# Gated linear attention in a two-layer trunk: the decay of all tokens made during the projections and loaded by chunk

## What is computed

```python
proj = h @ w_in                          # q, k (4 heads x 128), v, g_out (1024 each), a_lr (16)
log_a = log_sigmoid(a_lr @ w_gate2 + b_gate) / 16
# by chunk of tokens, per head:
bcum = cumsum(log_a, within the chunk)
o_inter = (q * exp(bcum)) @ state
attn[t, s] = sum_d q[t, d] * k[s, d] * exp(bcum[t, d] - bcum[s, d])     # s <= t
o = o_inter + attn @ v
k_dec = k * exp(bcum[last] - bcum)
state = exp(bcum[last]) * state + k_dec.T @ v
y = rms_norm(o) * silu(g_out) @ w_out
```

## Time and profile before

| | |
|---|---|
| median of 3 runs | 2583.39 us (2582.79 to 2583.41) |
| the profiled execution | 2580.99 us; span 2579.2 us |
| PE | 2521.8 us busy, 98% |
| DVE | 1721.7 us, 67% |
| POOL | 1287.0 us, 50% |
| ACT | 1106.3 us, 43% |
| TensorE clock granted | 0.998 of full |
| from the first product of chunk 0 to that of chunk 1 | 209.32 to 241.48 us |
| chunks 1 to 6 | 27.4 to 27.6 us each |

### The profile page before, as it was taken

How to read it: one execution, slowest core, us unless ns; L and a number is a source line. 1 busy time by engine, 2 the same in 40 slices (tenths; PEclk the granted TensorE clock), 3 DMA queues, 4 the chain that set the end, 5 groups by cost and what they waited for, 6 DMA issues and landing times.

```text
span 2579.2 us, 33641 instructions
## 1 busy us (share of the span) xinstructions
PE 2521.8 (98%) x11752; PEld 2087.3 (81%) x11752; DVE 1721.7 (67%) x2209; ACT 1106.3 (43%) x1952; POOL 1287.0 (50%) x985
## 2 busy tenths in 40 slices
PE   8999998989999999999999999999999999999998
PEld 6787887878888888887888888888877888888886
DVE  5125667986877865577665899965677777656556
ACT  4116666553333344455333333344544333334444
POOL 3125445555555555445666455544454555555543
PEclk9999999999999999999999999999999999999999
DMA  6665224425665648664888455587633656326764
GB/s 229 207 209 164 80 84 148 162 86 196 220 216 201 216 150 310 193 204 143 287 296 258 139 184 184 172 302 255 214 110 117 214 203 218 130 70 208 268 193 147
DMA packets 305517, 489.30 MB, mean 190 GB/s; under 512 B 32274, under 2 KB 128147, under 8 KB 305364
## 3 DMA queue, kind: packets, MB, share of 16 engines
q1 hardware_dynamic: 305364, 487.32, 56.7%
HBM read 326.15 MB, written 152.70 MB: 186 GB/s over the span
## 4 chain that ended last, share of the span: by engine, by line
PE 83%; issue 6%; DVE 4%; POOL 3%; ACT 2%; DMA 1%; SPq 0%; POOLq 0%; DVEq 0%; ACTq 0%
PE ps L617 27%; PE ps L619 26%; PE ps L618 26%; PE ps L2599 2%; POOL ebuf L1187 1%; POOL ebuf L1186 1%; PE ps L2458 1%; DVE r_all L1787 1%; DMA stage<-in_a_w_in 1%; DVE r_all L1762 1%; POOL g_sb L1197 1%; DVE xl_all L1769 0%; POOL w_lo_main L612 0%; DVE n_all L1800 0%; DVE s_ring L703 0%
## 5 line engine op out<-in xcount | busy, mean ns | idle before, releaser
L685 POOL TENSOR_TENSOR ring_lo<-stg,ring_hi 128x512 fp32r<-128x512 f32 x682 | 976.8, 1435 | 920.1 <-ACT ring_hi L681 919.7
L681 ACT ACTIVATE ring_hi<-stg 128x512 fp32r<-128x512 f32 x682 | 429.9, 631 | 1059.3 <-PE ps L619 993.0
L617 PE MATMUL ps<-xh_all,ring_hi 128*128 128x512 f32 x1568 | 614.3, 392 | 8.2 <-issue 5.1
L619 PE MATMUL ps<-xh_all,ring_lo 128*128 128x512 f32 x1568 | 610.8, 390 | 0.0
L618 PE MATMUL ps<-xl_all,ring_hi 128*128 128x512 f32 x1568 | 610.6, 389 | 0.0
L703 DVE TENSOR_TENSOR s_ring<-s_stage,s_ring 128x512 fp32r<-128x512 f32 x242 | 301.8, 1259 | 228.3 <-ACT s_ring L699 228.0
L617 PE MATMUL ps<-ring_hi,s_ring 128*128 128x512 f32 x1064 | 415.9, 391 | 2.7 <-DVE r_all L1787 1.6
L619 PE MATMUL ps<-ring_hi,s_ring 128*128 128x512 f32 x1064 | 414.4, 390 | 0.0
L618 PE MATMUL ps<-ring_lo,s_ring 128*128 128x512 f32 x1064 | 414.3, 389 | 0.0
L617 PEld LDWEIGHTS ps<-xh_all,ring_hi 128*128 128x128 f32 x1568 | 294.5, 188 | 69.9 <-issue 9.1
L619 PEld LDWEIGHTS ps<-xh_all,ring_lo 128*128 128x128 f32 x1568 | 294.4, 188 | 61.5
(11 more groups left out here) (227 smaller groups left out, 3531.7 us busy)
## 6 DMA issues: line engine op xcount, KB each, us to landing
s_stage<-h_scratch SPq DMA_DIRECT2D x238, 256.0 KB, 3.4
stg<-t_scratch SPq DMA_DIRECT2D x200, 256.0 KB, 3.0
h_scratch<-r_all SPq DMA_DIRECT2D x34, 1024.0 KB, 5.1
h_scratch<-r_all SPq DMA_DIRECT2D x80, 256.0 KB, 3.1
stg<-in_w_ffn_gate SPq DMA_DIRECT2D x34, 512.0 KB, 4.2
stg<-in_w_ffn_up SPq DMA_DIRECT2D x34, 512.0 KB, 5.6
stg<-in_w_ffn_down SPq DMA_DIRECT2D x66, 256.0 KB, 3.5
t_scratch<-r_all SPq DMA_DIRECT2D x28, 512.0 KB, 2.8
```

What stands on the lines that cost most here:

```text
L617: pe.matmul(bank, s_hi, m_hi, start=first, stop=False, skip_group_check=more)
L619: return pe.matmul(bank, s_lo, m_hi, start=False, stop=last, skip_group_check=more)
L681: nc.scalar.activation(weight_slot(ring_hi, g), weights(g), ACT.Copy).then_inc(wh_done, 1)
L685: nc.gpsimd.tensor_tensor(weight_slot(ring_lo, g), weights(g), f32(weight_slot(ring_hi, g)), ALU.subtract).then_inc(wl_done, 1)
```

## The change

The decay of all tokens is made during the projections, in eight tiles `u` of one head and 512 tokens, channels on the partitions. After products 11, 13, ... 25 PE does one fp32r matmul of 96 rows (high and low parts of `a_lr` and of the gate weights stacked; the bias no longer rides on a row of ones). One product later DVE adds the bias and takes the minimum with 0, and ACT does absolute value, exponential and logarithm; two products later DVE combines them and sums along the tokens with a scan that restarts every 128 tokens (`resets` has a 0 there); three products later SP stores the tile to `decay_scratch`. In the chunk loop `gate_logits`, `cumulate`, exp/ln, the subtraction and the copy are gone, and SP loads `bcum` of a chunk (4 heads x 128 x 128) ahead of `qk`. That of chunk 0 is loaded behind the last copies' stores and blocks 40 to 43.

```diff
@@ SP, projections
+                    if q == 0:
+                        sp.wait_ge(normed, 7)
+                        for r in range(6):
+                            sp.dma_start(wg_stage[r * RANK:(r + 1) * RANK, :], a_w_gate2[0]).then_inc(const_ld, 16)
+                    if q - 3 in GATE_AT:
+                        u = GATE_AT[q - 3]
+                        sp.wait_ge(cum_done, u + 1)
+                        sp.dma_start(bc_d[u % H, :, half(u // H)], decay_sum[:, :]).then_inc(bc_stored, 16)
...
             for b in range(40, 44):
                 load_block(sp, b)
-            sp.wait_ge(z_ready, 1)
-            chunk_loads(CH, "al")
+            sp.wait_ge(bc_stored, 16 * 8)
+            chunk_loads(0, "bc")
@@ SP, chunk
                 sp.wait_ge(g_ready, of(c, 2, 2))
-                if not isinstance(c, int) or c < NC - 2:
-                    chunk_loads((c + 2) * CH, "al")
                 chunk_loads(after, "xc")
                 sp.wait_ge(qk_decayed, of(c, 2, 2))
                 sp.wait_ge(z_done, of(c, NL, NL))
                 sp.wait_ge(level_ready, of(c, NL + 1, 1))
+                chunk_loads(after, "bc")
                 chunk_loads(after, "qk")
@@ POOL, chunk
-                pool.wait_ge(bcum_done, c + 1)
+                pool.wait_ge(bc_ld, of(c, 16, 16))
@@ ACT, projections
+            def softplus(u):
+                act.wait_ge(z_min, u + 1)
+                wait(act, log_a_done, u - 1)
+                nc.scalar.activation(soft2[:, u % 2, :], ps[:, u % 4, :], ACT.Abs, bias=b_gate[:, u % H:u % H + 1],
+                                     scale=GLA_TAU).then_inc(z_abs, 1)
+                act.wait_ge(z_abs, u + 1)
+                nc.scalar.activation(soft2[:, u % 2, :], soft2[:, u % 2, :], ACT.Exp, scale=-1.0).then_inc(z_exp, 1)
+                act.wait_ge(z_exp, u + 1)
+                nc.scalar.activation(soft2[:, u % 2, :], soft2[:, u % 2, :], ACT.Ln, bias=1.0).then_inc(z_soft, 1)
...
-                    if m == 3 and j == 4:
-                        act.wait_ge(al_ld, 16)
-                        exp_abs(0)
-                        softplus(0)
+                    if 8 * m + j - 1 in GATE_AT:
+                        softplus(GATE_AT[8 * m + j - 1])
                     if m % 2:
@@ DVE, projections
+            def gate_sum(u):
+                dve.wait_ge(z_soft, u + 1)
+                dve.wait_ge(z_min, u + 1)
+                nc.vector.scalar_tensor_tensor(out=decay[:, u % 2, :], in0=soft2[:, u % 2, :], scalar=-1.0 / GLA_TAU,
+                                               in1=decay[:, u % 2, :], op0=ALU.mult, op1=ALU.add).then_inc(log_a_done, 1)
+                dve.wait_ge(log_a_done, u + 1)
+                dve.wait_ge(consts_set, 4)
+                wait(dve, bc_stored, 16 * u)
+                nc.vector.tensor_tensor_scan(decay_sum[:, :], resets[:, :], decay[:, u % 2, :], 0.0, ALU.mult, ALU.add
+                                             ).then_inc(cum_done, 1)
@@ PE, projections
-                    if q == 28:
-                        pe.wait_ge(const_ld, 16 * 6)
-                        pe.wait_ge(ones_ld, 16)
-                        gate_logits(0)
-                    if q == 31:
-                        cumulate(0)
...
                     mm.then_inc(proj_ready, 1)
+                    if q in GATE_AT:
+                        gate_logits(GATE_AT[q])
@@ PE, chunk
-                if not last:
-                    gate_logits(c + 1)
...
-                if not last:
-                    cumulate(c + 1)
...
                 if not last:
                     pe.wait_ge(qk_decayed, of(c, 2, 2))
+                    pe.wait_ge(state_done, of(c, H, 2))
```

More of the change, by code:

```diff
@@ L623, in x_slot @@
             return (x_in if t % 4 < 2 else x_more)[:, t % 2, :]
+        GATE_AT = {11 + 2 * u: u for u in range(8)}
+        b_gate, b_gate_16 = dev[:, 0:H], dev[:, H:2 * H]
         def level(ap, b):
@@ L736, in _ @@
             sp.dma_start(gnorm_bc[:, :], a_g_norm[0].partition_broadcast(P)).then_inc(const_ld, 16)
[L737 to L739 removed]
+            sp.dma_start(b_gate, a_b_gate[0].rearrange("(h p) -> p h", p=P), allow_slow_non_contiguous=True).then_inc(const_ld, 16)
             def chunk_loads(col, which):
                 cols = bass.ds(col, CH)
[L743 to L744 removed]
+                if which == "bc":
+                    sp.dma_start(bcum[:, :].rearrange("p (h t) -> p h t", h=H), bc_d[:, :, cols].rearrange("h p t -> p h t")
+                                 ).then_inc(bc_ld, 16)
                 elif which == "xc":
@@ L1632, in _, with al_rest, gate_min @@
             nc.vector.memset(att[:, :, :], 0.0).then_inc(state_done, 1)
[L1634 to L1639, removed]
+            def al_rest():
+                dve.wait_ge(wa_hi_done, 2)
+                nc.vector.tensor_tensor(wg_parts[4 * RANK:, :], wg_stage[4 * RANK:, :], f32(wg_parts[4 * RANK:, :]),
+                                        ALU.subtract).then_inc(al_lo_done, 1)
+                for h in range(HALVES):
+                    dve.wait_ge(al_copied, 2 * h + 3)
+                    nc.vector.scalar_tensor_tensor(
+                        out=al_parts[2 * RANK:4 * RANK, half(h)], in0=ps[0:2 * RANK, 2 * h, :], scalar=1.0 / GLA_TAU,
+                        in1=f32(al_parts[0:2 * RANK, half(h)]), op0=ALU.mult, op1=ALU.subtract).then_inc(al_lo_done, 1)
+            def gate_min(u):
+                dve.wait_ge(z_ready, u + 1)
+                nc.vector.tensor_scalar(decay[:, u % 2, :], ps[:, u % 4, :], b_gate_16[:, u % H:u % H + 1], 0.0,
+                                        ALU.add, ALU.min).then_inc(z_min, 1)
+            def gate_sum(u):
[8 more added lines that the diff above has]
+                                             ).then_inc(cum_done, 1)
             def scale_q(c):
@@ L1661, in _ @@
                     nc.vector.tensor_copy(evac[:, q % 4, :], ps[:, 4 + q % 4, :]).then_inc(v_copied, 1)
-                if m == 3 and j == 4:
-                    dve.wait_ge(al_ld, 16)
-                    log_sigmoid(0)
+                if q == 9:
+                    al_rest()
+                if q - 1 in GATE_AT:
+                    gate_min(GATE_AT[q - 1])
+                if q - 2 in GATE_AT:
+                    gate_sum(GATE_AT[q - 2])
                 if q % 3 == 0 and q:
@@ L1708, in chunk @@
                     keep(n)
-                    if n == 3 and not last:
-                        log_sigmoid(c + 1)
                     if n == 4:
@@ L2288, in _, with gate_logits @@
                 norm_turn(t)
[L2290 to L2294, removed]
-                pe.matmul(ps[:, 2, :], al_c[:, :], w_gate2[:, :], start=True, stop=True).then_inc(z_ready, 1)
-            def cumulate(c):
-                pe.wait_ge(log_a_done, c + 1)
-                for h in range(H):
-                    mm = pe.matmul(ps[:, 3, tile(h)], log_a[:, tile(h)], causal[:, :], start=True, stop=True)
-                mm.then_inc(cum_ready, 1)
+            def gate_logits(u):
+                if u == 0:
+                    pe.wait_ge(al_copied, 1 + 2 * HALVES)
+                    pe.wait_ge(al_lo_done, 1 + HALVES)
+                if u >= 4:
+                    pe.wait_ge(z_abs, u - 3)
+                pe.matmul(ps[:, u % 4, :], wg_parts[:, tile(u % H)], al_parts[:, half(u // H)], start=True, stop=True
+                          ).then_inc(z_ready, 1)
             for m in range(4):
```

78 lines of the change are left out of this document (30 added, 48 removed).

## The result

The changed kernel takes 2591.95 us (median of 6 runs, 2589.23 to 2594.54) against 2583.26 us of the kernel before beside it: ratio 1.0031, interval 1.0020 to 1.0042. It is slower by 8.7 us, where 1.6 us faster was predicted. Its profiled execution has a span of 2587.6 us, 8.4 more than the 2579.2 of before.

What follows compares the result with a forecast made beforehand. PE, busy 98% of the span, was taken as the bound, with POOL setting chunk 0's pace. Chunk 1's later start, +9.8 (2.8 from late copies), and the loop's -11.4 gave -1.6 us: 2581.8 us, range 2573.5 to 2590.5.

Steps and rivals of the forecast that it cites:

- PE's 1.94 us per chunk: Chunk loop: PE loses the gate matmul, 1.05 us, and four running-sum matmuls, 0.89; chunks 1 to 6 can give 11.6.
- PE's projections: Projections: gate matmuls add 2.0 us, 3.2 go before product 31; chunk 0 1.2 sooner if nothing else is late.
- The six early softplus: First three quarters of the projections: costed at nothing, since copies lay ahead of PE; up to 4.47 us each without cover.
- The copies: End of projections: two softplus of 4.47 us delay ACT's copies; PE waits before products 30 and 31, chunk 0 +2.8.
- the start of the chain stays: Last quarter of projections: PE's 1.5 us delay was set against 1.6 us of small loads that SP no longer issues.
- Rival A: End of projections: slack in ACT's chain and an early decay landing; -7.6 us, 2575.8 us in all; chance 0.24.
- The issue of the first decay load: Chunk 0: issued 3.14 us after its first product, at 215.2; POOL starts at 222, 11.3 later; chunk 1 +9.8.
- the upper bound: Chunk 0's decay landing: SP moves 5.3 MB from 206.6 us at 299 GB/s, until 224 us.
- The loop: Chunks 1 to 6: each gives 1.9 us (0.9 to 2.4), together -11.4 us (-5.4 to -14.4).
- most of the delay has cover: Chunk loop: qk comes 0.4 to 1.0 us later; about 0.7 is covered by DVE's 0.76 idle before merging level 0.
- rival B: Every chunk: decay load and POOL's exponents push DVE's first level past its cover; +6.8 us, 2590.2; chance 0.14.
- Rival C: Products 30 and 31: matmuls at 1.2 GHz after PE's waits, 4.8 us in product 31; 2586.6 us; chance 0.09.

Runs made afterwards that it cites:

- e1: Changed kernel with ACT's copy of a product out of PSUM put ahead of the softplus; 2580.54 us, ratio 0.9992 to the kernel before.
- e2: Changed kernel with chunk 0's decay load issued behind product 29's store, ahead of chunk 0's qk; 2586.98 us, ratio 1.0016 to the kernel before.
- e4: Changed kernel with chunk 0's decay load moved only ahead of weight blocks 40 to 43, behind all stores; 2588.23 us, ratio 1.0020.
- e8: Changed kernel with only chunk 0's decay load moved to mid-projections, once its four tiles are stored; 2584.21 us, ratio 1.0002.
- e9: Changed kernel with one edit: in the chunk loop qk is loaded before the decay; 2588.23 us, ratio 1.0018 to the kernel before.
- e11: Changed kernel with only the last softplus moved behind the copy of product 26; 2586.53 us, ratio 1.0011 to the kernel before.
- e7: Changed kernel with copies ahead of softplus, qk ahead of decay in the loop, chunk 0's decay loaded mid-projections; 2572.23 us, ratio 0.9950.

## Why the prediction was wrong, by its steps

**Right.** PE's 1.94 us per chunk are gone, and the whole of it can be had: with qk first a middle chunk gives 27.40 - 25.42 = 1.98 us. PE's projections came as costed: without late copies chunk 0 starts 1.7 us sooner (e1), 1.2 was predicted. Softplus takes 4.46 to 4.47 us (4.47 predicted; the terms that I wrote out add to 4.42, the 4.47 is the difference of the two starts), enters the last quarter's chain twice, and PE waits before products 30 and 31. The six early softplus were hidden: from 45.77 us, where the early wait of the earlier trace rows ends, to 196.96 PE waits for nobody. The scan took 1.22 us in seven of the eight tiles, within its bounds, and 2.21 in one, and cost nothing. POOL's start holds chunk 0 back in after, which e2, e4 and e8 show. The Trainium skill (ScalarE: Activation LUTs, "What ACT_TABLE_LOAD costs") would have had a drain of about 1.38 us more with each switch of table set. The trace doesn't agree: the table load starts 0.02 us behind the end of the activation before it (196.41 and 196.43), and from its start to the exponential it is again 1.29 us (197.72), as in the trace of before.

**The copies, +3.7 us.** I wrote "the start of the chain stays", since PE's 1.5 us of gate matmuls were set off against two small loads. It didn't stay: the copy of product 24 is 6.05 us later, which is a softplus (4.47) and 1.58. In e1, where no softplus stands in the chain, the copies of 24, 26 and 27 are still 1.44, 1.68 and 1.84 later than before: this is the part that I had set off. At the copy of 26 the delay in after is 11.06 = 2 x 4.47 + 1.58 + 0.54; at that of 27 it is 12.51, since of the two blocks issued at 202.23 the second landed 1.39 us behind the first, where both were there before. 1.58 + 0.54 + 1.45 = 3.6: the term was right in its mechanism, and chunk 0's start 3.7 too early. Rival A, a slack in ACT's chain, had no part in it.

**The issue of the first decay load, +3.3 us.** I kept the 3.14 us between chunk 0's start and the issue from the trace of before. It became 6.42; with the copies ahead of softplus it is 3.85 (e1). With the copies late, the stores, a unit's load, a decay tile, qk and the unit's store fall into one burst: from 210 to 222 us the DMA share is 0.94, and the issue of product 30's store, 1.50 us in before, took 3.56. I had used the stage's rate for a bound on the landing and not for SP's issue. The landing itself was nearer than feared: 6.20 us from issue to use, where I took 6.8. But the 224 us that I had called the upper bound was none: POOL started at 228.40, and less the 3.7 of the copies that is still 224.7. Together POOL started 17.65 us later than before, not 11.3 (3.7 + 3.3 - 0.6); 1.15 came back, 1.5 was taken. So chunk 1 started 16.5 later instead of 9.8: 6.7 of the 10 us that I missed.

I let chunk 0's end hang on POOL's start alone. That overlooked the weight blocks, which came level with the decay already in before: ACT's second exponential ends at 213.95, the cut of block 40 follows at 214.06, and the next one waits for its block:

```profile
214.06 0.63 ACT L606 ACTIVATE w_hi_main<-stage 128x512 fp32r<-128x512 f32 x1
215.53 0.63 ACT L606 ACTIVATE w_hi_main<-stage 128x512 fp32r<-128x512 f32 x1 [0.83 <-DMA stage<-in_a_w_in]
```

In after the decay is the later of the two. With it out of the way (e8) 6.4 of the 16.5 us come back, and the other 10.1 stay.

**The loop, +2.5 us.** I took 1.9 per chunk within 0.9 to 2.4; it is 1.48. I had written that "most of the delay has cover" in DVE's 0.76 us of idle time. qk is used 0.9 to 1.0 us later in the chunk (0.6 in the first), which is the size I had, but the cover was too small by the 0.3 to 0.5 us that PE waits before the first level. This is rival B's mechanism, at a smaller price. The order of the two loads alone gives it back (e9). The other 0.8 us lie in chunk 7 and behind GLA. Chunk 7's 0.6 may be the same order: it lasts 31.1 to 31.4 us in the kernels with the decay ahead, 30.7 to 31.1 with qk ahead (30.80 before). For the 0.2 there is no cause on record, and they are below what single spans tell.

**Rival C** was there and not where it counted: product 30 ran at 0.50 to 0.54 of the clock behind the wait of 3.88 us and took 8.5 us instead of 5.6, but PE would have waited for the copy of product 27 anyway. The slow product also shortened the wait before product 31 to 0.86 us, and the clock held there. Where that wait was longer the rival came true: e11 (3.45 us), e4 (2.64) and e8 (2.56) pay 1.4 to 1.6 us for it, a third of the 4.8 that I had written, since the lower clock lasted some 3 us and not the whole product. That after didn't pay it at product 31 is luck. In chunk 0 the clock was 0.84 against 0.95; as its end is set by ACT, POOL and the loads, no run here tells what that cost.

## What to carry to other kernels

An activation with its table loads that is put ahead of a copy delays everything that follows from the copy's store; put it behind the copy. Ask of a new load two things: from when its data exist, here some 75 us before the load was issued, and what stands behind it in the queue, here qk, on which the next chunk hangs. When a change makes several transfers late, don't carry their old spacing over: here they came as a burst, in which issuing itself took longer (3.56 us for one store).

## What the runs showed of the hardware

Issuing a 256 KB store on SP's queue took 0.34 us at 200.81, after 3.9 us with a DMA share of 0.00, and 3.56 us at 215.52, in a stretch with a share of 0.94. The other transfers issued in that stretch took 0.34 to 0.96 us each, so the share alone doesn't give the time; what does isn't shown here. The same store took 1.50 us in before, 2.82 in e1 and 4.29 in e7.

In the kernels with late copies, waits of 3.88 (after), 3.45 (e11), 2.64 (e4) and 2.56 us (e8) before a product were followed by the lower of PE's two clock levels, 1.2 of 2.4 GHz (granted 0.50 to 0.55), for some 6, 3, 3 and 3 us; waits of 1.37 (e2), 1.27 (e9) and 0.86 us (after) weren't (granted 1.00, and 5.57 to 5.58 us for the product). The length of the wait doesn't decide alone: the 0.88 us at 217.30 in before was followed by the longer ones of the earlier trace rows.

The scan over 128x512 took 1.22 us, against 0.67 of an elementwise sum of that shape in the same stretch:

```profile
201.06 1.23 DVE L1658 TENSOR_TENSOR_SCAN decay_sum<-resets,decay 128x512 f32<-128x512 f32 x1
202.20 0.67 DVE L1669 TENSOR_TENSOR n_all<-n_all 128x512 f32<-128x512 f32 x1
```

The Trainium skill (DVE: opcode table, instruction layouts, handler registers and perf-mode slots, "Datapath and trigger behaviour") says that the scan runs at half throughput; the trace agrees, at 1.8 times.
